# A two-layer hybrid decoder step: layer one's input projection in half-size products, with its weight sums made ahead in layer zero

## The reference

```python
def rglru_mixer(x, conv_buf, h0, w_in, conv_w, conv_b, ga_w, ga_b, gx_w, gx_b, lam, w_out):
    gx = jnp.einsum('bsd,de->bse', x, w_in)
    gate, xr = jnp.split(gx, 2, axis=-1)
    xc, new_buf = causal_dwconv(xr, conv_buf, conv_w)
    xc = xc + conv_b
    h, h_last = rglru(xc, h0, ga_w, ga_b, gx_w, gx_b, lam)
    y = jnp.einsum('bsc,cd->bsd', jax.nn.gelu(gate, approximate=True) * h, w_out)
    return y, new_buf, h_last
```

## Time and profile before

| | |
|---|---|
| runs shown | 1385.75, 1387.11, 1387.92 us (median 1387.11) |
| the profiled execution | 1385.73 us, of which its span 1383.9 us |
| TensorE busy | 1334.0 us, 96% of the span |
| VectorE, ScalarE, GpSimd busy | 543.2, 217.5, 122.2 us |
| chain that ended last, by engine | PE 86%, DMA 9%, ACT 2%, DVE 2% |
| granted TensorE clock | 0.998 of full speed |
| DMA | 472.49 MB, mean 341 GB/s |

### The profile page before, as it was taken

How to read it: one execution, slowest core, us unless ns; L and a number is a source line. 1 busy time by engine, 2 the same in 40 slices (tenths; PEclk the granted TensorE clock), 3 DMA queues, 4 the chain that set the end, 5 groups by cost and what they waited for, 6 DMA issues and landing times.

```text
span 1383.9 us, 20214 instructions
## 1 busy us (share of the span) xinstructions
PE 1334.0 (96%) x8632; PEld 888.8 (64%) x8632; DVE 543.2 (39%) x1161; ACT 217.5 (16%) x385; POOL 122.2 (9%) x138
## 2 busy tenths in 40 slices
PE   8999999999999999998899999999999999999896
PEld 7888875656555565664488888666555555566552
DVE  5677766331111211331346888642221111223217
ACT  0000114001010000100134553310101001010012
POOL 0000001111000110121010000010011100111100
PEclk9999999999999999999999999999999999999999
DMA  9800469999999999999992113899999999999995
GB/s 380 308 5 1 172 277 355 414 425 426 426 427 426 426 425 426 425 424 425 388 327 100 61 61 122 305 396 426 425 427 425 426 427 426 426 426 423 426 402 219
DMA packets 68594, 472.49 MB, mean 341 GB/s; under 512 B 16494, under 2 KB 27374, under 8 KB 40847
## 3 DMA queue, kind: packets, MB, share of 16 engines
q1 hardware_dynamic: 52061, 449.90, 78.4%
q0 software_dynamic: 11520, 15.52, 3.2%
q10 hardware_dynamic: 4922, 5.74, 1.4%
HBM read 468.38 MB, written 27.32 MB: 358 GB/s over the span
## 4 chain that ended last, share of the span: by engine, by line
PE 86%; DMA 9%; ACT 2%; DVE 2%; issue 1%; POOL 0%; ACTq 0%; POOLq 0%; SPq 0%; DVEq 0%
PE ps L1105 28%; PE ps L1141 15%; PE ps L782 10%; PE ps L737 9%; PE ps L836 7%; PE ps L1068 7%; DMA ring<-in_moe_w_down 3%; DMA ring<-in_moe_w_up 3%; PE ps L1055 3%; PE ps L1129 1%; PE ps L1079 1%; PE ps L853 1%; DMA ring<-yrows 1%; DMA yrows<-A,Bt 1%; PE ps L1246 1%; ACT A L1474 1%
## 5 line engine op out<-in xcount | busy, mean ns | idle before, releaser
L1105 PE MATMUL ps<-ring,A 128*64 128x256 f32 x4096 | 456.1, 380 | 15.0 <-DMA ring<-in_moe_w_gate 6.8
L1105 PEld LDWEIGHTS ps<-ring,A 128*64 128x64 f32 x4096 | 326.7, 137 | 155.0 <-issue 39.5
L1141 PE MATMUL ps<-ring,A 128*64 128x512 f32 x1024 | 233.9, 597 | 7.1 <-issue 1.1
L2069 DVE TENSOR_TENSOR A<-A,ps 128x256 f32<-128x256 f32 x64 | 26.9, 421 | 537.8 <-PE ps L1105 537.8
L1141 PEld LDWEIGHTS ps<-ring,A 128*64 128x64 f32 x1024 | 75.8, 136 | 119.6 <-issue 113.3
L737 PE MATMUL ps<-A,ring 128*128 128x260 f32 (+2 forms) x576 | 130.1, 387 | 0.3 <-DMA ring<-in_a_w_in 0.3
L737 PEld LDWEIGHTS ps<-A,ring 128*128 128x128 f32 x576 | 110.1, 193 | 18.5 <-DMA ring<-in_a_w_in 1.0
L672 POOL DMA_INDIRECT A<-x,idx x42 | 44.5, 1060 | 672.6 <-PE ps L1055 624.4
L1068 PE MATMUL ps<-C,Bt 104*64 104x512 f32 x400 | 95.7, 620 | 0.0
L2072 DVE COPY A<-ps 128x256 f32<-128x256 f32 x64 | 27.1, 424 | 123.6 <-PE ps L1129 123.6
L1469 ACT ACTIVATE A<-ps 128x512 f32<-128x512 f32 x42 | 25.1, 597 | 304.2 <-PE ps L1141 304.2
(11 more groups left out here) (298 smaller groups left out, 1133.2 us busy)
## 6 DMA issues: line engine op xcount, KB each, us to landing
ring<-in_moe_w_gate SPq DMA_DIRECT2D x62, 2048.0 KB, 23.5
ring<-in_moe_w_up SPq DMA_DIRECT2D x60, 2048.0 KB, 25.1
ring<-in_moe_w_down SPq DMA_DIRECT2D x60, 2048.0 KB, 26.6
ring<-yrows SPq DMA_DIRECT2D x10, 1024.0 KB, 9.8
ring<-in_a_w_in SPq DMA_DIRECT2D x6, 1536.0 KB, 23.2
ring<-in_moe_w_down SPq DMA_DIRECT2D x8, 1024.0 KB, 27.1
ring<-in_b_w_in SPq DMA_DIRECT2D x8, 1024.0 KB, 12.9
ring<-in_moe_w_up SPq DMA_DIRECT2D x6, 1024.0 KB, 43.1
```

Of the source, the lines that this page charges most:

```text
L1105: mm = pe.matmul(ps[hf * ROWS:(hf + 1) * ROWS, (GATE_BANK, 3)[u], :FH], xgT[:, k, :], ring[:, slot, col:col + FH], start=(k == 0), stop=(k ...
L1141: mm = pe.matmul(ps[nh * ROWS:(nh + 1) * ROWS, 2, :], hidT[:, at:at + ROWS], ring[:, slot, m * D + nh * 512:m * D + (nh + 1) * 512], start ...
L2069: tt(gated, gated, ps[:, 3, :FH], ALU.mult).then_inc(ready, 1)
```

## The change

1. Layer one's chunks 1 to 7 take seven half-size products each (28 matmuls in place of 32), by the scheme of layer zero: the block rows are the two halves of the contraction, the block columns are the gate and the convolution's input. Chunk 0 stays as it was.
2. The sums of weight blocks that the scheme needs ("forms") are made on VectorE in layer zero (`weight_form`, four operations for a chunk, seven chunks). SyncE's queue fetches 1 MB of raw weights per chunk into a free slot, waits for VectorE, writes the forms to DRAM and waits for that, ahead of the first expert loads. In layer one a chunk's load is 0.75 MB raw and 1 MB of forms; the array of weights is laid out anew by the host.
3. Layer one's ring slots 0, 1, 8, 9 serve the chunks twice. The first three expert loads of layer one, which came at chunks 2, 4 and 6, now wait for the last chunk (`ROOM`).
4. VectorE makes the token pieces for the scheme (16 operations before chunk 1) and seven sums per chunk out of PSUM, which replace ScalarE's two copies. ScalarE takes the first convolution tap, the square of a and the square of the gate. `recurrence` of chunk c-2 stands ahead of `conv` of chunk c-1, and the two gate products of a chunk stand apart among the next chunk's products.
5. The sums of output weights move to the end of VectorE's iterations 1 (two q), 2 and 3.

The core of the diff:

```diff
+OUT_SUMS_AT = {1: (0, 1), 2: (2,), 3: (3,)}
+PARTS = (1, 6, 7, 5, 3, 4, 2)
+FORM_UNITS = {4: (1,), 5: (2, 3), 7: (4,), 8: (5, 6)}
-ROOM = ((6, 6, 6, 6, 6, 6, 8, 8, 9, 10), (1, 2, 3, 4, 5, 6, 7, 8, 9, 9))
+ROOM = ((6, 6, 6, 6, 6, 6, 8, 8, 9, 10), (8, 8, 8, 8, 9, 10, 11, 12, 13, 13))
...
+                def put_back(c):
+                    sp.wait_ge(form_ok, c)
+                    sp.dma_start(forms_dram[c], stage(c)).then_inc(forms_out, 16)
+                    sp.wait_ge(forms_out, 16 * c)
...
+                put_back(6)
+                put_back(7)
...
                     for c in range(1, KT):
-                        for jj in range(2):
-                            pe.wait_ge((ev_a[1], ev_b[1])[jj], c)
-                            input_product(c, jj, 0)
-                            if c == 1 and jj == 0:
-                                pe.wait_ge(ev_b[1], 1)
-                            input_product(c, jj, 1).then_inc(mm_in[1], 1)
-                        rg_gates(c - 1)
+                        for i in PARTS[:5]:
+                            in_product(c, i)
+                        rg_gate(c - 1, 0)
+                        in_product(c, PARTS[5])
+                        rg_gate(c - 1, 1)
+                        in_product(c, PARTS[6])
...
-                for n in range(4):
-                    early_part(n)
-                if l == 1:
-                    rg_gates(KT - 1)
-                for n in range(4, len(EARLY)):
+                for n in range(len(EARLY)):
+                    if l == 1 and n in (4, 5):
+                        rg_gate(KT - 1, n - 4)
                     early_part(n)
...
+                    for c in range(1, KT + 1):
+                        if c < KT:
+                            first_product(c)
+                        first_tap(c - 1)
+                        gate_square(c - 1)
+                        if c == KT:
+                            early_copies(0, 3)
+                        decay(c - 1)
+                        gelu(c - 1)
+                        if c == KT:
+                            early_copies(3, 4)
+                        input_gate(c - 1)
...
+            def weight_form(c):
+
+                dve.wait_ge(stage_in, 16 * c)
+                a11, a12, a22, a21 = (stage(c)[:, n_ * BLOCK:(n_ + 1) * BLOCK] for n_ in range(4))
+                step(tt(a22, a21, a22, ALU.add))
+                step(tt(a21, a11, a21, ALU.subtract))
+                step(tt(a11, a22, a11, ALU.subtract))
+                tt(a12, a12, a11, ALU.subtract).then_inc(form_ok, 1)
...
+                    for c in range(1, KT + 2):
+                        if 2 <= c <= KT:
+                            for what, i in (("u4", 5), ("c22", 5), ("c12", 3), ("c21", 4), ("c11", 2)):
+                                in_sum(c - 1, what, i)
+                        if c == KT:
+                            conv(c - 1)
+                        if c >= 2:
+                            recurrence(c - 2)
+                        if c < KT:
+                            conv(c - 1)
+                            in_sum(c, "u2", 6)
+                            in_sum(c, "u3", 7)
+                        if c <= KT:
+                            gate_cube(c - 1)
+                        if c >= 2:
+                            out_pieces(1, c - 2)
+                        if c <= KT:
+                            root_of(c - 1)
+                            gated_input(c - 1)
+                        for q in OUT_SUMS_AT.get(c, ()):
                             for add in (out_s1, out_s2, out_s3):
-                                add(1, c - 2)
-                    recurrence(KT - 1)
+                                add(1, q)
...
                 if l == 0:
-                    for add in (out_s1, out_s2):
-                        for q in range(KT // 2):
-                            add(0, q)
+                    for q in range(KT // 2):
+                        out_s1(0, q)
+                    weight_form(KT - 1)
+                    for q in range(KT // 2):
+                        out_s2(0, q)
```

More of the change, by code:

```diff
@@ L178, in room_count @@
             return (0, freed_after(POS_IN[1] - 1))[l] + ROOM[l][pos - POS_EXP[l]]
+    if POS_IN[1] <= pos < POS_EXP[1]:
+        return freed_after(max(p for p in range(pos) if ring_slot(p) == ring_slot(pos)))
     return freed_after(pos - RING)
@@ L244, in build, with stage @@
         pad = C[:, 9 * T:10 * T + WB - 1]
-        def g1_tile(c):
-            return tmp[8] if c < KT - 1 else pad[:, :T]
+        two = ring[:, 2, 2 * D:]
+        gelus = (two[:, :T], tmp[8])
+        in_u2, in_u3, in_u4 = (two[:, T + n * HALF:T + (n + 1) * HALF] for n in range(3))
+        in_p1 = [ring[:, s, RAW + FORMS:RAW + FORMS + HALF] for s in (0, 1)]
+        def stage(c):
+            return ring[:, STAGED[c], :FORMS]
         xk = [C[:TT, i * D:(i + 1) * D] for i in range(NT)]
@@ L335, in build @@
                   + [ring[:, 6 + n // 3, W3 + (n % 3) * HALF:W3 + (n % 3 + 1) * HALF] for n in range(6)])
+        in_pieces = ([ring[:, SCRATCH[1][1], n * HALF:(n + 1) * HALF] for n in range(15) if n != len(EARLY) + 2]
+                     + [two[:, T + n * HALF:T + (n + 1) * HALF] for n in (3, 4)])
         def out_part_w(l, m, kh):
@@ L571, in _ @@
                     rows_back(0)
-                    for m in range(KT // 2):
-                        input_unit1(m)
-                    pos = POS_IN[1] + KT // 2
+                    for c in range(KT // 2):
+                        input_unit1(c)
+                    pos = POS_IN[1] + KT
                     room(pos)
@@ L595, in _ @@
                     sp.dma_start(nb_s[0, :, 0:2, :], a["state_conv_b"][0, :, 1:3, :]).then_inc(state_out, 16)
+                    weight_forms()
+                else:
+                    for c in range(KT // 2, KT):
+                        input_unit1(c)
                 for e in range(NE):
@@ new lines, in _ @@
+                    act.wait_ge(lam_ok, 3)
+                    act.wait_ge(pad_ok, 2)
+                    for jj, out in enumerate((pad[:, WB - 1:], tmp[0])):
+                        act.wait_ge(mm_in[1], jj + 1)
+                        for part, (lo, hi) in enumerate(FIRST_COLS):
+                            ins = act.activation(out[:, lo:hi], ps[:, jj + 2 * part, :hi - lo], ACT.Copy)
+                        ins.then_inc(ev_a[1], 1)
+                    for c in range(1, KT + 1):
[10 more added lines that the diff above has]
+                        input_gate(c - 1)
@@ L1706, in _ @@
                 add_parts(u)
+                for n_ in FORM_UNITS.get(u, ()):
+                    weight_form(n_)
                 for n_ in range(2):
@@ new lines, in _ @@
+                    dve.wait_ge(xT_act, NT)
+                    for k in range(KH):
+                        t1, t2, t3, t4 = (in_pieces[4 * t + k] for t in range(4))
+                        b = [[token_part(a_, hf)[:, k, :] for hf in range(2)] for a_ in range(2)]
+                        step(tt(t1, b[0][1], b[0][0], ALU.subtract))
+                        step(tt(t2, b[1][1], t1, ALU.subtract))
+                        tt(t3, b[1][1], b[0][1], ALU.subtract)
+                        ins = tt(t4, b[1][0], t2, ALU.subtract)
```

290 lines of the change are left out of this document (172 added, 118 removed).

## The result

| | before | after |
|---|---|---|
| median (14 runs each) | 1386.55 us | 1389.69 us |
| lowest to highest | 1384.62 to 1388.46 | 1387.84 to 1392.65 |
| ratio to before | | 1.0028 (95%: 1.002 to 1.0035) |

The account below looks back on a forecast made before the run. TensorE was taken to bound layer one's projection, and weight loads too at the end of layer zero's experts. -12.3 + 8.6 + 0.9 + 1.5 = -1.3 us against a 1387.11 us median gave 1385.8 us, range 1379.5 to 1391.

Parts of the forecast that it names:

- Removed: 12.3 us: Layer one's projection: chunks 1 to 7 lose one half-size product each on TensorE, 7 x 1.754 = 12.28 us.
- Put back by the sums: 8.6: Layer one's chunks 2 to 4: output-weight sums on VectorE lengthen the loop, returning 8.6 us as TensorE waits.
- So the loop just fits into TensorE's 14.03: Layer one, per chunk: the chain through TensorE, ScalarE and VectorE takes 14.0 us, against TensorE's 14.03.
- -3.7: Layer one's output projection starts 3.7 us earlier, relative to the projection's start.
- The tail: 0.9 us: End of layer one's projection: a TensorE wait for a bank plus some 0.15 at the first router product, 0.9 us.
- The forecast wait of 0.75 us: Layer one's tail: TensorE waits 0.75 us for the bank of the second gate.
- 9.6: Layer one's tail: chunk 6's recurrence ends 9.6 us after TensorE's last projection product.
- Layer zero: 1.5 us: Layer zero's output sums: the seventh form, 2.88 us on VectorE less 1.33 spare, delays the first router product 1.5 us.
- that rival: Layer zero's queue: the last forms' write lands late, delaying expert loads; landing at 12 us adds 6.1 us; chance 0.11.
- Costs put at nothing: Token pieces, six forms, extra weight loads and three moved expert loads hide under other work: 0, loads at most 0.5 us.
- -1.3 forecast: Whole kernel: sum of -12.3, +8.6, +0.9 and +1.5 us, predicted as no change.

Follow-up runs that it names:

- experiment 1: Changed kernel with layer one's output-weight sums moved ahead of the root and gated input on VectorE, in the same chunks; 1380.45 us, 0.9962 of the changed kernel.
- experiment 3: Changed kernel with a one-column tanh on ScalarE ahead of the last chunk's wait for the recurrence, so the table loads earlier; 1386.08 us, ratio 1.0002.
- experiment 12: Kernel before, with only layer one's first three expert loads held until four output-projection products are done; 1386.08 us, ratio 0.9992.
- experiment 8: Changed kernel with output-weight sums ahead of the root, earlier tanh table, earlier chunk 7 form, and unread TensorE products (fillers) before both layers' first rows; 1378.12 us.

## Why the prediction was wrong

- **Removed: 12.3 us. Put back by the sums: 8.6.** Right. The waits stand in chunks 2 to 4 at the lines named, and moving the sums gave 8.5 us (experiment 1).
- **"So the loop just fits into TensorE's 14.03."** A size that was off: the loop is 14.1 to 14.2 us, in experiment 1 too, and about 0.6 more with the tap on VectorE, so the chain and not TensorE sets it. Six loops make some 0.9 us of the 1.0 that the stretch to the output projection missed (-2.7 for -3.7).
- **"The tail: 0.9 us."** The step that failed. The forecast wait of 0.75 us was 2.06. The recurrence was in time: it ended 9.75 us after TensorE's last projection product (836.07 - 826.32), where the prediction has 9.6, a figure whose working it doesn't show. I counted ScalarE's two table loads per chunk as covered by its idle time, which holds in the loop; in the last chunk the load stands behind the wait for the recurrence and in front of the tanh: 1.28 us (experiment 3). With it hidden the wait is 0.81 and the tail costs 1.16. At full clock it cost 2.4, and 4.0 where the clock fell.
- **The clock.** Nothing in the prediction allowed for it. The trace of before had no stretch of TensorE's work under full clock, and I priced pauses at their length. The pause of 2.06 us cost 1.6 more behind it, in some executions and not in others.
- **Layer zero: 1.5 us.** Right: 1.48. The last store of the forms landed in 3.83 us, so that rival did not come.
- **Costs put at nothing.** Pieces, six forms and three moved loads: right (TensorE has no wait ahead of chunk 1's first products nor in layer zero's projection; experiment 12 has the loads). Layer one's rows are the exception: 0.7 us later, and 1.5 more by the clock. The prediction has no term for them. The row write there is 1.3 us longer; a packet of the instruction queue beside it goes with that in all 17 traces, but that it is the cause is not shown.

By the table: -1.3 forecast, +1.0 loop, +2.6 tail, +2.2 end of layer one, -1.0 at the start, which is chance (23.18 and 23.5 in two variants of the kernel before) and hides as much of the miss: 3.5.

## What to carry to other kernels

Work put on the engine that closes a loop costs its length or nothing, by whether it stands behind or ahead of that engine's own wait in the loop: here three lines moved were worth 8.5 us. Where a chain runs out, go through every instruction that its overlap had hidden, table loads first. And price a new pause of the busiest engine above its own length, or close it.

## What the runs showed of the hardware

- TensorE's clock fell to half for 3.4 us behind pauses of 2.06 to 2.49 us, in two of three traces of the same kernel, and cost 1.6 us of a stretch that TensorE bounds and nothing where VectorE bounds. With the variants it fell behind the tail's pause of 2.06 to 2.07 in 3 of 7 traces, and behind chunk 2's of 2.48 to 2.49 in 5 of 9.
- At layer zero's rows it fell in three of the 15 traces without fillers there, behind waits of 0.8 to 1.0 us that left it up in others, and cost 0.6 us; one of the three is experiment 12, the kernel before.
- At layer one's rows it fell in 10 of 11 traces of the changed kernel and its variants without fillers there (waits of 1.3 to 2.2 us), in none of four of the kernel before and its variants (0.7 to 0.8). TensorE's end took 18.6 us where it was low for 3.4 us, 19.9 to 20.1 where for 6.8, and 17.0 to 17.1 where it stayed up. With fillers it stayed up in both traces; in one of them, experiment 8, the row write was as late as in the others (7.67 us).
- In the last chunk the 1.28 us table load stood behind the wait of the activation that needed it; a tanh of one column, 0.20 us, ahead of that wait brought it forward.
- An indirect row write took 7.6 to 8.0 us in all 12 traces in which a packet of the queue "instruction" (16 KB, 1.1 us) started 5 to 6 us into it, and 6.4 to 6.6 in the five without.
